# Norm stages of an encoder kernel: one tile at a time with three under way, instead of turns of two tiles

## The chip, the cores and the metric

The kernel runs on one core of one Trainium2 chip. The metric is the device time of one execution in microseconds (us). The core has a matmul engine (TensorE, PE in the rows; PEld is its weight load), a vector engine (VectorE, DVE), a scalar engine (ScalarE, ACT), GpSimd (POOL), and SyncE (SP), which here issues all DMA transfers. Each engine runs its own instructions strictly in order; they meet through semaphores. An instruction that waits holds up all that is queued behind it on its engine.

## The reference, cut to what matters

Two encoder layers run on a prompt of 1024 tokens and a sample of 256 tokens, width 1024, all in float32. Between mixer and MLP the reference norms the sublayer's output, adds it to the residual and norms again:

```python
def rms_norm(x, g, eps=EPS):
    xf = x.astype(jnp.float32)
    y = xf * lax.rsqrt(jnp.mean(xf * xf, -1, keepdims=True) + eps)
    return (y * g.astype(jnp.float32)).astype(x.dtype)
...
        h = rms_norm(x, p['norm_mix_pre'][layer])
...
        x = x + rms_norm(mix, p['norm_mix_post'][layer])
        h = rms_norm(x, p['norm_ffn_pre'][layer])
        f = jnp.square(jax.nn.relu(h @ p['w_ff1'][layer])) @ p['w_ff2'][layer]
        x = x + rms_norm(f, p['norm_ffn_post'][layer])
```

## The kernel before, in words

The 1280 tokens are ten tiles of 128 tokens (partitions) by 1024 features. The kernel is a list of stages, each a block that all engines enter and leave together. Five of the stages are calls of `residual_norm` (L117 to L285), named by tags: norm0 (in front of the input projections; it only norms `x`), norm1, norm2 and norm3 (norm of the sublayer's output, residual add, norm, in one stage), and norm4 (the last residual add; it only does the first half and writes the outputs). In the trace their tiles are called `norm_...` whatever the tag. The other stages, which hold the large matmuls, are not touched.

The tensor `X` (`top_acc`) holds all ten tiles in SBUF. For one tile the full stage does this, in this order:

- ACT squares the sublayer's output with a row sum (L193) and takes the root (L197); DVE takes the reciprocal (L250) and multiplies the tile by it and by the post weight `gpost` (L252); POOL adds the old residual `x_old` (L232), which SP has loaded; SP stores the new residual.
- ACT squares and takes the root again (L207, L211); DVE takes the reciprocal (L258) and scales the rows into `h` (L260); PE turns the eight 128x128 blocks of `h` into PSUM (L282, `norm_ps`); DVE multiplies by the pre weight `gpre`, one value per partition now that the tile is turned, into `h_out` (L267); ACT rounds `h_out` to the high part of the matmul operand (L218); POOL subtracts to make the low part (L239).

The matmuls of the next stage take high and low part, three products for one float32 product.

The order is set by code: `in_turns` runs a hardware loop over turns of two tiles, and in each turn every engine does `begin` (the second norm's root and rows) of turn i, `mixer` (first norm) of turn i+1 and `finish` (turning, high, low) of turn i, each for both tiles of the turn. The small vectors of sums, roots and reciprocals have two columns and are used again each turn. `x_old` is one buffer of two tiles: SP issues its next load when both of its tiles have been added (L153), and the store behind it (L154). norm0 has no mixer and norm4 has only the mixer. The DVE's first arithmetic waits for both weight loads (`n_gains`).

## Time and profile before

| | |
|---|---|
| median of 3 runs | 4993.93 us (4993.36 to 5001.96) |
| the profiled execution | 4994.65 us, its span 4992.9 us |
| PE busy in the span | 4310.9 us (86%) |
| DVE, ACT, POOL busy | 2223.3, 1361.1, 1131.2 us |
| norm0 | starts with the program, next stage's first DMA issue at 74.66 us |
| norm1, norm2, norm3 | from 2138.8, 3109.6, 3954.4 us to 2219.1, 3190.5, 4035.0 us |
| norm4 | from 4925.0 us to the end |

The five stages take about 384 us of the span together, and PE is busy for 76 of these. In the timeline rows a start and a length in us come first, then engine, source line, operation, output and inputs; "x2" is two instructions merged in one row, whose length spans both; what stands in brackets is how long the engine had been idle and what ended that. In the rows by stretch there stand, behind the length, busy time and count of PE, PEld, DVE, ACT and POOL, then the granted PE clock as a share of full speed, the DMA engines' busy share and GB/s. Since stages are separated by a meeting of all engines, a stage's length counts in full.

### The profile page before, as it was taken

Reading aid. Unit: us, or ns where it says so; the run is one execution under the profiler, and the core shown is the slowest. Engines: PE = TensorE matmul, PEld = TensorE weight load, DVE = VectorE, ACT = ScalarE, POOL = GpSimd, SP = SyncE. Lnnn points to the kernel's source line nnn. Section 1 sums busy time; section 2 is a strip of 40 time slices with the busy share of each in tenths; the row PEclk is TensorE's granted clock in tenths of the full one; section 3 lists DMA queues with packets and bytes.
Section 4 is the critical chain, followed back from the end, with each engine's and each line's share of the span. In section 5 each row is a group of like instructions: output and inputs, shape, how many; then the busy total and the mean of one; then the engine's idle time right before and its main releaser. Section 6 shows DMA issues by size and latency. Waiting matters only on the chain. (4 is left out here: it accounts for less than half of the span.)

```text
span 4992.9 us, 65205 instructions
## 1 busy us (share of the span) xinstructions
PE 4310.9 (86%) x24458; PEld 3684.1 (74%) x24458; DVE 2223.3 (45%) x3245; ACT 1361.1 (27%) x2203; POOL 1131.2 (23%) x588
## 2 busy tenths in 40 slices
PE   4989786989999997849999998479999769999994
PEld 3867665888888886738888887357777658888883
DVE  3633044655665555733433443434444233433443
ACT  3211054343333333232111111323333221111111
POOL 2111033343333333351111111400000141111112
PEclk7999767999999998969999999689999879999997
DMA  2222276111111111131111110300000121111102
GB/s 74 73 80 73 64 249 229 52 42 42 59 42 55 42 45 59 45 122 34 42 34 42 35 41 21 98 20 5 5 5 34 47 93 34 42 34 42 40 27 88
DMA packets 211119, 288.09 MB, mean 58 GB/s; under 512 B 36688, under 2 KB 153680, under 8 KB 211040
## 3 DMA queue, kind: packets, MB, share of 16 engines
q1 hardware_dynamic: 211040, 287.05, 17.6%
q8 instruction: 48, 0.79, 0.1%
q14 instruction: 31, 0.25, 0.0%
HBM read 208.37 MB, written 77.99 MB: 57 GB/s over the span
## 5 line engine op out<-in xcount | busy, mean ns | idle before, releaser
L617 DVE TENSOR_TENSOR top_acc<-top_acc,ffn_bank 128x512 f32<-128x512 f32 x640 | 439.9, 687 | 400.0 <-PE ffn_bank L109 400.0
L107 PE MATMUL ffn_bank<-hT_ffn_high,ffn_w_high 128*128 128x512 f32 (+1 forms) x1536 | 545.4, 355 | 32.4 <-DVE ffn_w_low L594 32.4
L108 PE MATMUL ffn_bank<-hT_ffn_low,ffn_w_high 128*128 128x512 f32 (+1 forms) x1536 | 544.9, 355 | 0.0
L109 PE MATMUL ffn_bank<-hT_ffn_high,ffn_w_low 128*128 128x512 f32 (+1 forms) x1536 | 544.8, 355 | 0.0
L108 PE MATMUL ffn_bank<-ffn_w_low,ffn_f_high 128*128 128x512 f32 x1280 | 498.5, 389 | 0.0
L107 PE MATMUL ffn_bank<-ffn_w_high,ffn_f_high 128*128 128x512 f32 x1280 | 498.5, 389 | 0.0
L109 PE MATMUL ffn_bank<-ffn_w_high,ffn_f_low 128*128 128x512 f32 x1280 | 498.1, 389 | 0.0
L609 DVE TENSOR_TENSOR ffn_square<-ffn_relu 128x512 f32<-128x512 f32 (+1 forms) x192 | 146.5, 763 | 662.5 <-ACT ffn_relu L562 662.5
L107 PEld LDWEIGHTS ffn_bank<-hT_ffn_high,ffn_w_high 128*128 128x128 f32 x1536 | 291.4, 190 | 74.6 <-issue 33.2
L232 POOL TENSOR_TENSOR top_acc<-top_acc,norm_x_old 128x1024 f32 (+1 forms) x40 | 111.4, 2804 | 996.6 <-DVE top_acc L252 949.0
L108 PEld LDWEIGHTS ffn_bank<-hT_ffn_low,ffn_w_high 128*128 128x128 f32 x1536 | 291.5, 190 | 41.5
L109 PEld LDWEIGHTS ffn_bank<-hT_ffn_high,ffn_w_low 128*128 128x128 f32 x1536 | 291.3, 190 | 40.3
L586 POOL TENSOR_TENSOR ffn_w_low<-ffn_w_raw,ffn_w_high 128x2048 fp32r<-128x2048 f32 x30 | 138.5, 4615 | 711.3 <-ACT ffn_w_high L568 711.3
L579 POOL TENSOR_TENSOR ffn_w_low<-ffn_w_raw,ffn_w_high 128x2048 fp32r<-128x2048 f32 x32 | 147.1, 4596 | 666.7 <-ACT ffn_w_high L557 666.7
L562 ACT ACTIVATE ffn_relu<-ffn_bank 128x512 f32<-128x512 f32 (+1 forms) x192 | 101.1, 527 | 650.5 <-PE ffn_bank L109 650.5
L109 PEld LDWEIGHTS ffn_bank<-ffn_w_high,ffn_f_low 128*128 128x128 f32 x1280 | 240.3, 188 | 50.0
L107 PEld LDWEIGHTS ffn_bank<-ffn_w_high,ffn_f_high 128*128 128x128 f32 x1280 | 240.4, 188 | 49.1
L108 PEld LDWEIGHTS ffn_bank<-ffn_w_low,ffn_f_high 128*128 128x128 f32 x1280 | 240.4, 188 | 48.8
L282 PE MATMUL norm_ps<-top_ident,norm_h 128*128 128x128 f32 x320 | 75.9, 424 | 221.9 <-DVE norm_h L260 221.9
L557 ACT ACTIVATE ffn_w_high<-ffn_w_raw 128x2048 fp32r<-128x2048 f32 x32 | 61.3, 1917 | 746.8 <-DVE top_acc L617 745.5
L282 PEld LDWEIGHTS norm_ps<-top_ident,norm_h 128*128 128x128 f32 x320 | 63.8, 224 | 233.6 <-DVE norm_h L260 233.6
L1715 POOL TENSOR_TENSOR scan_NM<-scan_NT,scan_both_levels 128x512 f32<-128x512 f32 x120 | 165.0, 1378 | 212.2 <-PE scan_ps L1330 212.2
(388 smaller groups left out, 9402.6 us busy)
## 6 DMA issues: line engine op xcount, KB each, us to landing
ffn_w_raw<-in_w_ff SPq DMA_DIRECT2D x64, 1024.0 KB, 5.1
s_x<-top_acc SPq DMA_DIRECT2D x15, 1024.0 KB, 8.2
norm_x_old<-s_x SPq DMA_DIRECT2D x15, 1024.0 KB, 6.2
s_tm_both<-prepare_tb SPq DMA_DIRECT2D x20, 512.0 KB, 6.8
s_fm_dir<-prepare_fd SPq DMA_DIRECT2D x20, 512.0 KB, 6.4
scan_tb<-s_tm_both SPq DMA_DIRECT2D x20, 512.0 KB, 3.6
scan_fb<-s_fm_both SPq DMA_DIRECT2D x20, 512.0 KB, 4.3
scan_fd<-s_fm_dir SPq DMA_DIRECT2D x20, 512.0 KB, 4.9
```

Source lines behind the costliest of these rows:

```text
L107: pe.matmul(out, stationary[0], moving[0], start=start, stop=False)
L108: pe.matmul(out, stationary[0], moving[1], start=False, stop=False)
L109: return pe.matmul(out, stationary[1], moving[0], start=False, stop=stop)
L232: pool.tensor_tensor(x, x, x_old[:, j:j + 1, :], ALU.add).then_inc(x_updated, 1)
L282: last = pe.transpose(ps[j][:, k, :], h[j][:, k * P:(k + 1) * P], ident[:, :])
L557: act.activation(w2_sb[0][:, :, :], w2_raw[:, :, :], ACT.Copy).then_inc(w2_high, 1)
L562: act.activation(relu[u % 2][:, 0:n], bank[u % 4][:, 0:n], ACT.Relu).then_inc(relu_done, 1)
L579: pool.tensor_tensor(w2_sb[1][:, :, :], w2_raw[:, :, :], w2_sb[0][:, :, :].bitcast(F32), ALU.subtract).then_inc(w2_low, 1)
L586: pool.tensor_tensor(w1_sb[1][:, :, :], w1_raw[:, :, :], w1_sb[0][:, :, :].bitcast(F32), ALU.subtract).then_inc(w1_low, 1)
L609: dve.tensor_tensor(square[u % 2][:, 0:n], relu[u % 2][:, 0:n], relu[u % 2][:, 0:n], ALU.mult).then_inc(squared, 1)
L617: dve.tensor_tensor(a, a, bank[4 + u % 4][:, :], ALU.add).then_inc(added, 1)
L1715: pool.tensor_tensor(NM[u % 2][:, :, :], NTc[q][:, :, :], bcm(both_levels[:, m, :], GR), ALU.mult).then_inc(s["masked"], 1)
```

## The change: what it does

The loops over turns are gone: each stage is written out for ten tiles. In step t every engine does the first norm of tile t+2, the second norm's root and rows of tile t+1, and the high and low part of tile t. Sums, roots and reciprocals have a column per tile. `x_old` is three buffers of one tile, each with a load semaphore of its own; all three loads are issued ahead, and each added tile frees one. The pre weight is loaded broadcast over the partitions (512 KB instead of 4 KB) and applied to the unturned rows, together with the reciprocal, in one scalar_tensor_tensor; the multiply behind the turning and `h_out` are gone. ACT makes the high part straight from PSUM, and DVE, not POOL, makes the low part from PSUM and the high part. POOL has only the residual add left.

```diff
-    mixed = g_post is not None
-    x_old = E.sb("x_old", [P, 2, D])
-    gpost = E.sb("gpost", [P, D])
-    gpre = E.sb("gpre", [P, KB])
+
+    mixed, pre = g_post is not None, g_pre is not None
+    AHEAD = 3
+    x_old = [E.sb(f"x_old{j}", [P, D]) for j in range(AHEAD)]
+    gpost, gpre = E.sb("gpost", [P, D]), E.sb("gpre", [P, D])
...
+            def load(t):
+                dst = x_old[t % AHEAD][:, :] if mixed else X[:, t, :]
+                sp.dma_start(dst, of(x_src, t)).then_inc(loaded[t % AHEAD], 16)
             if mixed:
                 sp.dma_start(gpost[:, :], g_post.partition_broadcast(P)).then_inc(gains, 16)
...
+                for t in range(AHEAD):
+                    load(t)
+            if pre:
+                if not mixed:
+                    load(0)
+                sp.dma_start(gpre[:, :], g_pre.partition_broadcast(P)).then_inc(gains, 16)
             if mixed:
...
+                for t in range(TILES):
+                    sp.wait_ge(x_updated, t + 1)
+                    if t + AHEAD < TILES:
+                        load(t + AHEAD)
+                    sp.dma_start(of(x_dst, t), X[:, t, :]).then_inc(stored, 16)
+                sp.wait_ge(stored, 16 * TILES)
             else:
...
+                for t in range(1, TILES):
+                    if t >= AHEAD:
+                        sp.wait_ge(loaded[t % AHEAD], 16 * (t // AHEAD))
+                    load(t)
...
+            def mix_root_of(t):
+                act.activation(squares[0][:, :], X[:, t, :], ACT.Square, accum_out=col(sq1, t)).then_inc(mix_squares, 1)
+                act.wait_ge(mix_squares, t + 1)
+                act.activation(col(rt1, t), col(sq1, t), ACT.Sqrt, bias=eps[:, :], scale=1.0 / D).then_inc(mix_root, 1)
+
+            def x_root_of(t):
+                if mixed:
+                    act.wait_ge(x_updated, t + 1)
+                else:
+                    act.wait_ge(loaded[t % AHEAD], 16 * (t // AHEAD) + 16)
+                act.activation(squares[1][:, :], X[:, t, :], ACT.Square, accum_out=col(sq2, t)).then_inc(x_squares, 1)
+                act.wait_ge(x_squares, t + 1)
+                act.activation(col(rt2, t), col(sq2, t), ACT.Sqrt, bias=eps[:, :], scale=1.0 / D).then_inc(x_root, 1)
+
+            def high(t):
+                act.wait_ge(turned, t + 1)
+                act.activation(hT[0][part(t)], ps[t % 2][:, :, :], ACT.Copy).then_inc(high_done, 1)
 
-            in_turns(act, begin, mixer, finish)
+            for t in range(-2, TILES):
+                if mixed and t + 2 < TILES:
+                    mix_root_of(t + 2)
+                if pre and 0 <= t + 1 < TILES:
+                    x_root_of(t + 1)
+                if pre and t >= 0:
+                    high(t)
...
+            if mixed:
+                for t in range(TILES):
+                    pool.wait_ge(loaded[t % AHEAD], 16 * (t // AHEAD) + 16)
+                    pool.wait_ge(mix_scaled, t + 1)
+                    pool.tensor_tensor(X[:, t, :], X[:, t, :], x_old[t % AHEAD][:, :], ALU.add).then_inc(x_updated, 1)
...
+            def mixer(t):
+                dve.wait_ge(mix_root, t + 1)
+                dve.reciprocal(col(rc1, t), col(rt1, t)).then_inc(mix_inverse, 1)
+                dve.wait_ge(mix_inverse, t + 1)
+                dve.scalar_tensor_tensor(X[:, t, :], X[:, t, :], col(rc1, t), gpost[:, :], ALU.mult, ALU.mult).then_inc(mix_scaled, 1)
+
+            def rows(t):
+                dve.wait_ge(x_root, t + 1)
+                dve.reciprocal(col(rc2, t), col(rt2, t)).then_inc(x_inverse, 1)
+                dve.wait_ge(x_inverse, t + 1)
+                if t >= 2:
+                    dve.wait_ge(turned, t - 1)
+                dve.scalar_tensor_tensor(h[t % 2][:, :], X[:, t, :], col(rc2, t), gpre[:, :], ALU.mult, ALU.mult).then_inc(h_ready, 1)
+
+            def low(t):
+                dve.wait_ge(high_done, t + 1)
+                dve.tensor_tensor(hT[1][part(t)], ps[t % 2][:, :, :], hT[0][part(t)].bitcast(F32), ALU.subtract).then_inc(low_done, 1)
...
+            dve.wait_ge(gains, 16 * (mixed + pre))
+            for t in range(-2, TILES):
+                if mixed and t + 2 < TILES:
+                    mixer(t + 2)
+                if pre and 0 <= t + 1 < TILES:
+                    rows(t + 1)
+                if pre and t >= 0:
+                    low(t)
...
+            if pre:
+                for t in range(TILES):
+                    pe.wait_ge(h_ready, t + 1)
+                    if t >= 2:
+                        pe.wait_ge(low_done, t - 1)
                     for k in range(KB):
-                        last = pe.transpose(ps[j][:, k, :], h[j][:, k * P:(k + 1) * P], ident[:, :])
+                        last = pe.transpose(ps[t % 2][:, k, :], h[t % 2][:, k * P:(k + 1) * P], ident[:, :])
                     last.then_inc(turned, 1)
```

The functions `in_turns`, `begin` and `finish` go. The two places of the order that matter most, each before and after:

DVE in norm2, from its first arithmetic on, before: `rc1` and `rc2` are the reciprocals of the first and the second norm, `h0` and `h1` the scaled rows of a turn's two tiles; L179 is the start of the loop.

```order
L250 RECIPROCAL norm2_rc1<-norm2_rt1 128x1
L252 SCALAR_TENSOR_TENSOR top_acc<-top_acc,norm2_rc1,norm2_gpost 128x1024
L250 RECIPROCAL norm2_rc1<-norm2_rt1 128x1
L252 SCALAR_TENSOR_TENSOR top_acc<-top_acc,norm2_rc1,norm2_gpost 128x1024
L179 UNCONDITIONAL_BRANCH
L179 ISA
L258 RECIPROCAL norm2_rc2<-norm2_rt2 128x1
L260 ISA
L260 TENSOR_SCALAR norm2_h0<-top_acc,norm2_rc2 128x1024
L257 REGISTER_ALU
L258 RECIPROCAL norm2_rc2<-norm2_rt2 128x1
```

DVE in norm2 after, from the same place on: tiles 0 and 1 mixed, rows of 0; then step 0 (mixer of 2, rows of 1, low of 0) and step 1's mixer.

```order
L217 RECIPROCAL norm2_rc1<-norm2_rt1 128x1
L219 SCALAR_TENSOR_TENSOR top_acc<-top_acc,norm2_rc1,norm2_gpost 128x1024
L217 RECIPROCAL norm2_rc1<-norm2_rt1 128x1
L219 SCALAR_TENSOR_TENSOR top_acc<-top_acc,norm2_rc1,norm2_gpost 128x1024
L223 RECIPROCAL norm2_rc2<-norm2_rt2 128x1
L227 SCALAR_TENSOR_TENSOR norm2_h0<-top_acc,norm2_rc2,norm2_gpre 128x1024
L217 RECIPROCAL norm2_rc1<-norm2_rt1 128x1
L219 SCALAR_TENSOR_TENSOR top_acc<-top_acc,norm2_rc1,norm2_gpost 128x1024
L223 RECIPROCAL norm2_rc2<-norm2_rt2 128x1
L227 SCALAR_TENSOR_TENSOR norm2_h1<-top_acc,norm2_rc2,norm2_gpre 128x1024
L231 TENSOR_TENSOR hT_attention_low<-norm2_ps0,hT_attention_high 128x8x128
L217 RECIPROCAL norm2_rc1<-norm2_rt1 128x1
```

The two mixers of a turn, which stood side by side, are now parted: each mixer is followed by the rows of the tile ahead of it, and each low part stands between a rows and the next mixer.

ACT in norm0 before, the loop over turns (`sq2`, `rt2` sum and root of the second norm); table loads are rows of their own.

```order
L207 ISA
L207 ACT_TABLE_LOAD
L207 ACTIVATE norm0_squares1,norm0_sq2<-top_acc 128x1024
L209 REGISTER_ALU
L207 ISA
L207 ACTIVATE norm0_squares1,norm0_sq2<-top_acc 128x1024
L209 REGISTER_ALU
L211 ACT_TABLE_LOAD
L211 ACTIVATE norm0_rt2<-norm0_sq2,norm0_eps 128x1 x2
L218 ISA
L218 ACTIVATE hT_first_high<-norm0_h_out0 128x8x128
```

ACT in norm0 after, from the stage's start.

```order
L188 ACT_TABLE_LOAD
L188 ACTIVATE norm0_squares1,norm0_sq2<-top_acc 128x1024
L190 ACT_TABLE_LOAD
L190 ACTIVATE norm0_rt2<-norm0_sq2,norm0_eps 128x1
L188 ACTIVATE norm0_squares1,norm0_sq2<-top_acc 128x1024
L190 ACTIVATE norm0_rt2<-norm0_sq2,norm0_eps 128x1
L194 ACTIVATE hT_first_high<-norm0_ps0 128x8x128
L188 ACTIVATE norm0_squares1,norm0_sq2<-top_acc 128x1024
L190 ACTIVATE norm0_rt2<-norm0_sq2,norm0_eps 128x1
L194 ACTIVATE hT_first_high<-norm0_ps1 128x8x128
```

Both table loads stood inside the loop; now both stand ahead of the first root, and none follows in the stage.

## Rows read from the trace of the kernel before

**Rows 1.** Stretches norm0, norm1, norm2 and norm4: length, busy time and count per engine.
```profile
0.00:74.60 74.60, 18.18 (x80) 16.35 (x80) 21.27 (x31) 34.61 (x48) 23.66 (x14) 0.76 0.22 71
2138.80:2219.10 80.30, 19.42 (x80) 15.82 (x80) 41.66 (x51) 37.48 (x70) 53.28 (x20) 0.51 0.42 137
3109.60:3190.50 80.90, 19.43 (x80) 15.82 (x80) 41.66 (x51) 37.47 (x70) 53.69 (x20) 0.53 0.43 136
...
4924.90:4992.90 68.00, 0.00 (x0) 0.00 (x0) 18.57 (x21) 13.89 (x30) 26.26 (x10) 0.51 0.50 162
```

**Rows 2.** Timeline, norm0: start, length, engine, line, what [idle before].
```profile
27.30 0.16 DVE L258 RECIPROCAL norm_rc<-norm_rt 128x1 f32<-128x1 f32 x1 [6.70 <-ACT norm_rt L211]
...
39.86 0.16 DVE L258 RECIPROCAL norm_rc<-norm_rt 128x1 f32<-128x1 f32 x1 [6.70 <-ACT norm_rt L211]
...
68.46 4.66 POOL L239 TENSOR_TENSOR hT_first_low<-norm_h_out,hT_first_high 128x1024 fp32r<-128x1024 f32 x2 [5.21 <-ACT hT_first_high L218]
...
74.66 4.70 SPq L315 DMA_DIRECT2D conv_tap<-in_gdn_conv  x5
```

**Rows 3.** ACT groups, norm0: count | busy, mean ns | idle before.
```profile
L207 ACT ACTIVATE norm_squares<-top_acc 128x1024 f32 (+1 forms) x10 | 10.6, 1055 | 1.0 <-ACT norm_squares L207 0.8
L207 ACT ACT_TABLE_LOAD x4 | 5.1, 1283 | 9.2 <-DMA top_acc<-in_x_prompt 9.1
L211 ACT ACT_TABLE_LOAD x4 | 5.1, 1283 | 0.1
L211 ACT ACTIVATE norm_rt<-norm_sq,norm_eps 128x1 f32<-128x1 f32 x10 | 2.4, 286 | 0.1
L207 ACT ACTIVATION_READ_ACCUMULATOR norm_squares<-top_acc 128x1 f32 x10 | 1.9, 186 | 0.0
```

**Rows 4.** Timeline, norm2, opening and steady loop.
```profile
3109.60 0.38 SPq L145 DMA_DIRECT2D norm_x_old<-s_x  x1
...
3116.90 0.16 DVE L250 RECIPROCAL norm_rc<-norm_rt 128x1 f32<-128x1 f32 x1 [7.16 <-DMA norm_gpre<-in_norm_mix_pre]
3117.10 1.28 DVE L252 SCALAR_TENSOR_TENSOR top_acc<-top_acc,norm_rc,norm_gpost 128x1024 f32<-128x1024 f32 x1
...
3118.49 1.28 DVE L252 SCALAR_TENSOR_TENSOR top_acc<-top_acc,norm_rc,norm_gpost 128x1024 f32<-128x1024 f32 x1
3118.55 5.72 POOL L232 TENSOR_TENSOR top_acc<-top_acc,norm_x_old 128x1024 f32<-128x1024 f32 x2 [58.99 <-DVE top_acc L252]
...
3138.37 0.16 DVE L258 RECIPROCAL norm_rc<-norm_rt 128x1 f32<-128x1 f32 x1 [4.07 <-ACT norm_rt L211]
...
3139.51 1.97 PE L282 MATMUL norm_ps<-top_ident,norm_h 128*128 128x128 f32 x8 [8.73 <-DVE norm_h L260]
...
3144.02 5.75 POOL L232 TENSOR_TENSOR top_acc<-top_acc,norm_x_old 128x1024 f32 x2 [2.32 <-DVE top_acc L252]
3145.17 2.35 DVE L267 TENSOR_TENSOR norm_h_out<-norm_ps,norm_gpre 128x1024 f32<-128x1024 f32 x2
...
3151.58 0.16 DVE L258 RECIPROCAL norm_rc<-norm_rt 128x1 f32<-128x1 f32 x1 [4.06 <-ACT norm_rt L211]
```

**Rows 5.** Timeline, norm4.
```profile
4933.72 6.74 POOL L232 TENSOR_TENSOR top_acc<-top_acc,norm_x_old 128x1024 f32 x2 [58.24 <-DVE top_acc L252]
...
4938.46 3.08 DVE L252 SCALAR_TENSOR_TENSOR top_acc<-top_acc,norm_rc,norm_gpost 128x1024 f32 x1
...
4959.73 4.63 POOL L232 TENSOR_TENSOR top_acc<-top_acc,norm_x_old 128x1024 f32 x2 [6.98 <-DMA norm_x_old<-s_x]
...
4987.26 0.39 SPq L159 DMA_DIRECT2D out<-top_acc  x1
```

**Rows 6.** DMA rate, norm4 and the end of ffn1, in 40 slices.
```profile
GB/s 0 145 420 347 5 0 0 0 0 0 59 356 285 420 95 0 0 74 318 240 416 169 0 0 123 344 287 420 40 0 78 207 266 392 273 0 0 332 275 0
```

**Rows 7.** DMA issues, whole run: count, KB each, us to landing.
```profile
conv_w_raw<-in_w_in_even SPq DMA_DIRECT2D x12, 512.0 KB, 4.5
```

**Rows 8.** Timeline, just before norm1.
```profile
2124.83 1.03 ACT L2062 ACTIVATE top_acc<-gate_ps 128x1024 f32<-128x1024 f32 x1 [10.20 <-PE gate_ps L109]
```

More of the change, by code:

```diff
@@ L187, in _ @@
         @block.scalar
         def _(act):
-            def mixer(i):
-                for j in range(2):
-                    act.wait_ge(mix_scaled, 2 * i + j + 1)
-                    act.sem_inc(tick, 1)
-                    act.activation(squares[0][:, :].unsqueeze(1), X[:, bass.ds(2 * i + j, 1), :], ACT.Square,
-                                   accum_out=sq1[:, j:j + 1]).then_inc(mix_squares, 1)
-                    act.wait_ge(mix_squares, 2 * i + j + 1)
-                for j in range(2):
-                    act.activation(rt1[:, j:j + 1], sq1[:, j:j + 1], ACT.Sqrt, bias=eps[:, :],
-                                   scale=1.0 / D).then_inc(mix_root, 1)
@@ L224, in _ @@
+            act.wait_ge(eps_set, 1)
+            for t in range(-2, TILES):
[5 more added lines that the diff above has]
+                    high(t)
         @block.gpsimd
         def _(pool):
-            def mixer(i):
-                pool.wait_ge(loaded, 16 * i + 16)
-                for j in range(2):
-                    x = X[:, bass.ds(2 * i + j, 1), :]
-                    pool.wait_ge(mix_scaled, 2 * i + j + 1 + 2)
-                    pool.sem_inc(tick, 1)
-                    pool.tensor_tensor(x, x, x_old[:, j:j + 1, :], ALU.add).then_inc(x_updated, 1)
@@ L234, in finish @@
-            def finish(i):
-                for j in range(2):
-                    part = (slice(None), slice(None), bass.ds((2 * i + j) * P, P))
-                    pool.wait_ge(high_done, 2 * i + j + 1)
-                    pool.sem_inc(tick, 1)
-                    pool.tensor_tensor(hT[1][part], h_out[j][:, :, :], hT[0][part].bitcast(F32),
-                                       ALU.subtract).then_inc(low_done, 1)
-            in_turns(pool, lambda i: None, mixer, finish)
+            if mixed:
[3 more added lines that the diff above has]
+                    pool.tensor_tensor(X[:, t, :], X[:, t, :], x_old[t % AHEAD][:, :], ALU.add).then_inc(x_updated, 1)
@@ L244, in _ @@
         @block.vector
         def _(dve):
-            def mixer(i):
-                for j in range(2):
-                    x = X[:, bass.ds(2 * i + j, 1), :]
-                    dve.wait_ge(mix_root, 2 * i + j + 1)
-                    dve.reciprocal(rc1[:, j:j + 1], rt1[:, j:j + 1]).then_inc(mix_chain, 1)
-                    dve.wait_ge(mix_chain, 2 * i + j + 1)
-                    dve.scalar_tensor_tensor(x, x, rc1[:, j:j + 1], gpost[:, :].unsqueeze(1), ALU.mult,
-                                             ALU.mult).then_inc(mix_scaled, 1)
@@ L255, in begin @@
-            def begin(i):
-                for j in range(2):
-                    dve.wait_ge(x_root, 2 * i + j + 1)
-                    dve.reciprocal(rc2[:, j:j + 1], rt2[:, j:j + 1]).then_inc(x_chain, 1)
-                    dve.wait_ge(x_chain, 2 * i + j + 1)
-                    dve.tensor_scalar(h[j][:, :].unsqueeze(1), X[:, bass.ds(2 * i + j, 1), :], rc2[:, j:j + 1],
-                                      None, ALU.mult).then_inc(h_ready, 1)
-            def finish(i):
-                for j in range(2):
-                    dve.wait_ge(turned, 2 * i + j + 1)
-                    dve.wait_ge(low_done, 2 * i + j + 1)
-                    dve.tensor_tensor(h_out[j][:, :, :], ps[j][:, :, :], bc(gpre[:, :], P), ALU.mult).then_inc(scaled, 1)
-                dve.wait_ge(scaled, 2 * i + 2)
```

85 lines of the change are left out of this document (13 added, 72 removed).

## The prediction

> **What bounds the kernel now.** I read the page first: PE is busy 86% of the span, so its idle seventh is what can be won. The view by stretches [rows 1] says where a good part of it lies: norm0, norm1, norm2 and norm4 take 74.6, 80.3, 80.9 and 68.0 us with at most 19.4 us of PE work each (norm3 is another of norm1's kind and within its range). All engines meet at a stage's end, so a microsecond off a stage is one off the program. No engine fills such a stage either: POOL, the fullest, has 53.7 of 80.9 us in norm2. Next the timelines, for what the stages wait on.
>
> In norm0 the same reciprocal comes at 27.30 and 39.86 [rows 2]: 12.6 us for a turn of two tiles. It is one chain through four engines, with DVE idle 6.7 us in front of that reciprocal and two table loads of 1.28 us in each of the four loop turns [rows 3]. In norm2 the turn is 3138.37 to 3151.58, 13.2 us [rows 4]. There POOL is the chain: two adds in 5.75 and later two subtractions, and everybody waits for it in turn. In norm4 POOL ends its two adds in 4.63 us, then stands idle 6.98 us for the reload of its single buffer [rows 5].
>
> One behaviour of the chip decides the rest. A DVE operation with two SBUF tensors of 1024 columns takes 1.28 us [rows 4], but 3.08 us when it starts at 4938.46; POOL's two adds ran from 4933.72 to 4940.46, and the DVE operation ended 1.08 us after them [rows 5]. So it stood still until POOL had finished. POOL pays likewise: two adds cost 4.63 us alone (2.3 each), 6.74 beside DVE. DVE's multiply that reads PSUM takes 2.35 us for two in the midst of POOL's adds [rows 4], so it isn't stopped. The Trainium skill says the same (SBUF — State Buffer, "Who interferes with whom"): a DVE instruction with two SBUF inputs and a GpSimd one that reads SBUF exclude each other for the whole instruction. By that rule, the trace agrees.
>
> **The change part by part.** Durations: mixer and rows 1.28 each, reciprocal with its waits 0.3 before the first and 0.1 between two large ones (3117.10 to 3118.49 is 1.39), transposes of a tile 2.0 [rows 4], square 1.06, read 0.19, root 0.29, so about 1.5 per root with its wait [rows 3], high from PSUM 1.05 [rows 8], low 1.2 (the nearest row is the multiply from PSUM with one SBUF tensor, 2.35 for two [rows 4]; bounds 1.1 and 1.3), add 2.3 alone, a semaphore between engines 0.1 to 0.2.
>
> *norm0.* Gone: six of eight table loads, POOL's subtractions, the multiply behind the turning. Added: rows grow from a multiply by a scalar to 1.28, beside ACT's work. POOL is empty, so nothing stops DVE. What is late next is the chain from high of tile t to high of t+2, since ACT does the root of t+2 right behind high of t: 1.5 root + 0.3 + 1.28 rows + 2.1 turning + 1.1 high = 6.3 for two tiles, 3.15 a tile. DVE needs 2.8 a tile, ACT 2.7, so neither is the bound; the 512 KB loads need about 1.3 at 420 GB/s [rows 6]. Start: before, ACT waits until 9.1 for the first 1 MB [rows 3]; half of it at 420 GB/s is 1.3 less, 7.8 (elsewhere 512 KB land 4.5 after their issue [rows 7], which fits). Two table loads, root and rows give 13.5, the first low ends at 18.1 (turning, the next root in between, high, low). The tenth ends at 18.1 + 9 x 3.15 = 46.5. Before, the last subtraction ends at 73.1 [rows 2]. Gain 26.6 (bounds 22, if half a microsecond more is lost per tile, and 30, if DVE's 2.8 is the pace).
>
> *norm1 to norm3, head.* The pre weight is now 512 KB and is issued behind three residual loads; DVE's first reciprocal waits for it. Before, with 1.5 MB in flight, it comes 7.3 us after the first issue [rows 4]. One MB more at 420 GB/s [rows 6] is 2.5: 9.8. Bounds 7.3 (the queue absorbs it) and 12.3 (half that rate). Then mixers 10.0 to 12.7; add of tile 0 to 15.0 and of 1 to 17.3; rows of 0, held up by the second add, to 18.4; mixer of 2 and rows of 1 to 21.3; add of 2 to 23.6.
>
> *Middle.* Count from the end of add t+1. DVE's mixer of t+2 was waiting for POOL and ends at 1.1. ACT's root of t+1 had to wait for that add, so rows of t+1 can't start before 2.1; POOL, which sees the mixer's semaphore at 1.3, comes first and holds its add to 3.6. Rows end at 4.7, low of t at 5.9. Mixer of t+3 runs 6.2 to 7.5; now the root for rows of t+2 is ready, and rows start 0.1 behind the mixer, before POOL, as 3118.49 stands before 3118.55 [rows 4]. They end at 8.9, low runs beside POOL, POOL's add ends at 11.2, and all begins again. So two tiles cost 11.2 instead of 13.2. Three such pairs bring add of tile 8 to 23.6 + 33.6 = 57.2. *Tail:* add of 9, rows of 8, low of 7, rows of 9, low of 8, transposes, high and low of 9: 12.1, so 69.3. Before, the stretches less the 1.5 from last arithmetic to next issue [rows 2] are 79.4 and 78.8 [rows 1]. Gain 10.1 and 9.5; three times 9.8 is 29.5.
>
> Register instructions of the loops cost nothing visible; POOL's subtractions go from POOL, where they lay on the chain, to DVE, where they lie beside its add. The residual stores (512 KB) end long before the tail does.
>
> *norm4.* Loads are ahead by three tiles, so the 6.98 us waits go; late next is the alternation of DVE and POOL at their shared access: 1.08 + 2.34 = 3.4 a tile. Head as before but with gpost issued first: mixers of 0 and 1 end at 9.4, add of 0 at 11.7, add of 8 at 11.7 + 8 x 3.42 = 39.1, add of 9 at 41.4. From the last store's issue to the end there are 5.6 us for 1 MB [rows 5]; half of it at 420 GB/s is 1.3 less, 4.3. End at 45.9 against 68.0 [rows 1]: gain 22.1. A load and a store per tile are 1 MB, 2.5 us at 420 GB/s and 3.7 at the 285 of middling slices [rows 6], so the loads hide; at 240, also seen there, 4.4 a tile, the gain would be 13.5.
>
> **Sum.** 26.6 + 29.5 + 22.1 = 78.2. From the profiled execution, 4994.65 (1.75 more than its span), that is 4916.4; the median stands 0.7 below it, so 4916.
>
> **The rivals.**
> *POOL first.* POOL always gets in between mixer and rows. The margin that I count on is 0.06 us, and rows has one more wait (for `turned`) than the reciprocal pair it is read from. Then each tile costs mixer 1.28 + 0.2 + add 2.34 + rows 1.08 + low 1.2 + 0.3 = 6.4, add of 2 ends at 22.4, the stage at 22.4 + 45 + 8.4 = 75.6. Three stages then win 10.6 instead of 29.5: 4935. The same page says that who starts first holds the ports to the end; so that order, which no row here fixes for rows against add, decides.
> *DVE first each time.* The pace falls to its floor 1.28 + 0.1 + 1.28 + 2.34 = 5.0 a tile, seven tiles win 4 us a stage, less what the tail takes back: 4906. Against it stands that the root of t+1 must follow the add.
> *The circle closes on each tile: slower.* Low of t holds DVE until ACT's high of t, which is queued behind the root of t+1, which waits for POOL's add, which waits for DVE. If that ring has to be gone round once a tile, it costs add 2.34 + root 1.75 + high 1.1 + low 1.2 + mixer 1.6 + rows 1.6 = 9.6, the stage 23.6 + 67.3 + 12.1 = 103, 24 more than before. Three stages lose 72 against 49 won in the others: 5018. It decides from 8.5 us a tile on. Against it: the code starts each add two tiles ahead, so the ring carries two tiles.
> *The DMA waits stay.* If weights come at 12.3 and norm4 goes by its transfers, 7.5 and 8.6 are lost: 4932.
>
> **How the numbers follow.** Alternating order as above 0.58; POOL first 0.2; DVE first 0.1; DMA waits 0.1; the slower ring 0.02. From 4906 I go down to 4895 for a pace in norm0 and heads at their lower bounds; 4938 takes in POOL first with a little more. A change under 0.2%, 10 us, can hardly be told from none here. All but the ring lie far beyond it, so faster has 0.96, no change 0.015, slower 0.025.
>
> **What would show it.** In norm0 rows repeat every 3.1 to 3.3 us and only two table loads stand at its head. In norm1 to norm3 the first reciprocal comes at about 9.8, the adds come in pairs, one of 2.3 and one of 3.6 to 3.8, and rows alternate between 1.28 and about 2.6; all adds at 2.4 and all rows at 2.6 or more would be POOL first. In norm4 no add waits for a load, and DVE's operations are 2 to 3.4 long. Wrong would be: a norm stage still near 79, or an untouched stage whose matmuls have other lengths than before.

## The result: faster, but just outside the range

The changed kernel took 4939.91 us (median of 4 runs, 4936.71 to 4948.69) against 4994.16 for the kernel before (4993.36 to 5001.96): a ratio of 0.9891, 95% interval 0.9874 to 0.9908. The forecast was 4916, with a range up to 4938, so the median lies 2 us outside it. The profiled execution took 4936.96 us, with a span of 4935.2.

The view by stretches shows where the time went. Columns are those of [rows 1]: length, then busy time and count of PE, weight loads, DVE, ACT and POOL, the granted clock, DMA share and GB/s. Of the changed kernel: norm0, the scan (the recurrences, which the change doesn't touch), norm1, norm2, norm3, norm4.

```profile
0.00:44.66 44.66, 18.55 (x80) 15.12 (x80) 26.00 (x31) 26.12 (x42) 0.20 (x4) 0.73 0.34 131
797.90:1958.40 1160.50, 1032.83 (x8080) 960.99 (x8080) 640.62 (x1030) 414.38 (x661) 422.13 (x319) 0.94 0.15 47
2124.06:2198.00 73.94, 19.69 (x80) 15.69 (x80) 60.11 (x51) 37.99 (x70) 23.45 (x10) 0.50 0.48 156
3088.20:3162.43 74.23, 19.68 (x80) 15.69 (x80) 60.12 (x51) 38.00 (x70) 23.47 (x10) 0.50 0.49 156
3926.40:4000.76 74.36, 19.67 (x80) 15.69 (x80) 60.12 (x51) 39.28 (x71) 23.47 (x10) 0.54 0.49 155
4890.44:4935.20 44.76, 0.00 (x0) 0.00 (x0) 33.28 (x21) 13.45 (x30) 23.41 (x10) 0.51 0.77 246
```

The scan of the kernel before, in the same view:

```profile
831.00:1973.00 1142.00, 1021.40 (x8080) 951.05 (x8080) 653.69 (x1030) 414.27 (x661) 425.75 (x319) 0.95 0.14 47
```

| stage | before | after | difference | forecast |
|---|---|---|---|---|
| norm0 | 74.6 | 44.7 | -29.9 | -26.6 |
| norm1, norm2, norm3 | 80.3, 80.9, 80.7 | 73.9, 74.2, 74.4 | -19.4 | -29.5 |
| norm4 | 68.0 | 44.8 | -23.2 | -22.1 |
| scan | 1142.0 | 1160.5 | +18.5 | 0 |
| all else | | | -3.7 | 0 |
| span | 4992.9 | 4935.2 | -57.7 | -78.2 |

Two things are to be explained: the middle norm stages won 10 us less than forecast, and a stage whose code nobody touched lost 18.5 us. The last stages are the smaller matter: "all else" is spread over the other stages, and such drifts come without a change too (the stage that prepares the tokens was 219.8 to 230.6 us long in the thirteen traces of this study, though no kernel touches it). That is why stage lengths, and not only medians, are compared below.

**The middle stages in the trace.** The timeline of norm2 after the change (start, length, engine, line, what) answers to [rows 4]; its head first, then one tile of the steady part and the start of the next:

```profile
3088.24 0.36 SPq L156 DMA_DIRECT2D norm_gpost<-in_norm_ffn_post  x1
...
3090.06 0.61 SPq L162 DMA_DIRECT2D norm_gpre<-in_norm_mix_pre  x1
...
3097.76 0.16 DVE L217 RECIPROCAL norm_rc<-norm_rt 128x1 f32<-128x1 f32 x1 [9.39 <-DMA norm_gpre<-in_norm_mix_pre]
...
3112.59 1.28 DVE L219 SCALAR_TENSOR_TENSOR top_acc<-top_acc,norm_rc,norm_gpost 128x1024 f32<-128x1024 f32 x1
...
3113.99 3.46 DVE L227 SCALAR_TENSOR_TENSOR norm_h<-top_acc,norm_rc,norm_gpre 128x1024 f32<-128x1024 f32 x1
3114.02 2.34 POOL L211 TENSOR_TENSOR top_acc<-top_acc,norm_x_old 128x1024 f32<-128x1024 f32 x1 [3.75 <-DVE top_acc L219]
...
3117.37 1.21 DVE L231 TENSOR_TENSOR hT_attention_low<-norm_ps,hT_attention_high 128x1024 fp32r<-128x1024 f32 x1
3118.51 0.14 DVE L217 RECIPROCAL norm_rc<-norm_rt 128x1 f32<-128x1 f32 x1
...
3120.08 3.46 DVE L227 SCALAR_TENSOR_TENSOR norm_h<-top_acc,norm_rc,norm_gpre 128x1024 f32<-128x1024 f32 x1
```

The head came out as forecast (first reciprocal 9.5 us after the first issue, 9.8 said). The steady part did not. The rows are recorded 0.03 us ahead of the add, the situation in which the forecast, counting on a margin of 0.06, gave them the shared access, and yet they last 3.46 us and the add 2.34: POOL had the access and DVE stood still. It is so on every steady tile, 6.09 us from rows to rows (3113.99 to 3120.08) instead of 5.6. All 40 adds of the program are short: in the page's list of groups (count | busy, mean ns | idle before)

```profile
L211 POOL TENSOR_TENSOR top_acc<-top_acc,norm_x_old 128x1024 f32<-128x1024 f32 x40 | 93.8, 2345 | 1041.2 <-DVE top_acc L219 1041.2
```

So the rival "POOL first" came true, at 6.1 us a tile instead of its 6.4. Its stage of 75.6 us ends with the last arithmetic; with the 1.5 us from there to the next issue [rows 2] it is 77.1, against 74 measured.

**The scan in the trace.** PE's waits within the scan (engine, what waited <- releaser: us in total, times, longest) begin after the change with the first row below; before the change the same matmuls, then in line 1274, had the second:

```profile
PE scan_ps L1240 <- issue: 25.0, 18, 2.9
```

```profile
PE scan_ps L1274 <- issue: 2.4, 9, 0.3
```

PE is ready and waits for nothing but its own next instruction. In each of nine turns the wait of 0.3 us is joined by one of 2.1 to 2.9 us: 22.6 us more in all. The page's list of DMA queues (packets, MB, share) shows what it fetches, first before, then after:

```profile
q8 instruction: 48, 0.79, 0.1%
```

```profile
q8 instruction: 122, 2.00, 0.2%
```

74 packets more, of 16 KB each. 71 of them fall in the scan, which has 85 instead of 14: some eight per turn.

### The profile page after: what moved, and what is told of

Its sections match the earlier page's. It is cut to its first block and busy times, and to the rows that moved or that the text cites. A ratio compares the mean times of both kernels' runs of the same rounds, so it can differ in the third digit from the quotient of the medians.

```text
span 4935.2 us, 64292 instructions
## 1 busy us (share of the span) xinstructions
PE 4316.5 (87%) x24458; PEld 3686.9 (75%) x24458; DVE 2285.7 (46%) x3245; ACT 1354.3 (27%) x2197; POOL 1013.3 (21%) x548
## 5 line engine op out<-in xcount | busy, mean ns | idle before, releaser
L107 PEld LDWEIGHTS ffn_bank<-hT_ffn_high,ffn_w_high 128*128 128x128 f32 x1536 | 291.3, 190 | 69.3 <-issue 27.9
L211 POOL TENSOR_TENSOR top_acc<-top_acc,norm_x_old 128x1024 f32<-128x1024 f32 x40 | 93.8, 2345 | 1041.2 <-DVE top_acc L219 1041.2
```

The costliest lines, as they stand in the source:

```text
L107: pe.matmul(out, stationary[0], moving[0], start=start, stop=False)
L211: pool.tensor_tensor(X[:, t, :], X[:, t, :], x_old[t % AHEAD][:, :], ALU.add).then_inc(x_updated, 1)
```

## The experiments

Theories: **A**, the change shifted PE's later code and the scan's loop came to lie badly; **B**, the scan lost time to something else. **C**, which of two instructions gets the shared access is a race of a few hundredths of a microsecond, which the recorded starts don't settle, and only operands in SBUF take part in it; **D**, POOL has it whatever is done, or another ring sets the pace. **E** and **F** are on the head, **G** and **H** on the load buffers. Stage lengths, in us:

| kernel | norm0 | scan | norm1, 2, 3 | norm4 | median, runs |
|---|---|---|---|---|---|
| changed kernel | 44.7 | 1160.5 | 73.9, 74.2, 74.4 | 44.8 | 4939.91, 4 |
| a_pad | 60.5 | 1142.5 | 73.9, 74.1, 74.1 | 44.6 | 4938.22, 4 |
| b_pad (of before) | 76.4 | 1158.9 | 80.4, 81.1, 80.8 | 68.0 | 5013.25, 5 |
| e_peloop | 44.7 | 1141.9 | 74.0, 74.1, 74.3 | 45.0 | 4923.15, 4 |
| c_late | 44.6 | 1163.4 | 68.1, 69.0, 68.4 | 42.2 | 4928.89, 4 |
| j_before_direct (of before) | 74.6 | 1141.8 | 85.0, 85.6, 85.4 | 67.1 | 5007.35, 8 |
| d_low | 71.9 | 1162.3 | 77.8, 77.9, 77.7 | 45.0 | 4983.17, 10 |
| f_low1 | 44.8 | 1165.8 | 66.2, 66.1, 66.2 | 45.1 | 4924.41, 4 |
| g_gains | 44.7 | 1163.8 | 69.1, 68.9, 69.0 | 44.8 | 4933.29, 4 |
| h_ahead1 | 44.6 | 1163.1 | 84.7, 83.7, 82.0 | 73.6 | 5005.00, 10 |
| i_ahead2 | 44.6 | 1160.0 | 72.8, 73.1, 72.7 | 44.9 | 4936.28, 4 |
| best | 44.6 | 1143.1 | 61.1, 61.2, 61.2 | 44.6 | 4883.11, 5 |

(norm0 is counted from the span's start to the next stage's first issue, as in [rows 1].) Beside these, the kernel before ran at medians of 4993.58 to 4996.94.

### Code position: a_pad, b_pad, e_peloop

a_pad, in PE's program of norm0, ahead of the turning:

```diff
+            if pre and not mixed:
+                for _ in range(165):
+                    pe.sem_inc(tick, 1)
```

> The changed kernel with 165 semaphore increments more on TensorE ahead of its work in the first norm stage, and nothing else, so that all of TensorE's later code stands 165 instructions further on. Theory A (the change shifted TensorE's code, and the scan's loop now touches a piece of code that has to be fetched again in each turn): with one more shift of that size the loop lies as before, the stage of the scan falls from 1158 to about 1140 us, the packets of the instruction queue from 122 to about 50, the time from 4937 to about 4920. Theory B (the scan lost its 18 us to something else, such as where the DMA engines' work falls or how the stage begins): the scan stays at 1158 within 1 and the time is the same, within 2 us.

Measured: the scan 1142.5, the queue 50 packets, as A said. But the time hardly moved (4938.22, ratio to before 0.9889, 0.9873 to 0.9906), which A had not said. The padding has a price of its own: norm0 is 15.8 us longer. The first transposes start at 28.24 instead of 12.43, since PE works through the increments only once the stage has begun.

```profile
28.24 3.65 PE L255 MATMUL norm_ps<-top_ident,norm_h 128*128 128x128 f32 x16 [28.24 <-issue]
```

The same in the kernel before, ahead of its transposes:

```diff
+            if not mixed:
+                for _ in range(91):
+                    pe.sem_inc(tick, 1)
```

> The kernel before with 91 semaphore increments more on TensorE ahead of its work in the first norm stage, which moves its later code about as far as the change did. Theory A (position of TensorE's code): the scan goes from 1140 to about 1158 us, the packets of the instruction queue from 48 to about 120, the time from 4994 to about 5012. Theory B (something else in the changed stages): no stage changes by over 1 us and the time is the same.

Measured: slower, ratio 1.0038 (1.0023 to 1.0052), scan 1158.9. With none of the change in it, the kernel before takes on the changed kernel's scan, its packets and its wait. The list of queues, PE's waits in the scan, and the first transposes, which started at 15.66 before:

```profile
q8 instruction: 121, 1.98, 0.2%
```

```profile
PE scan_ps L1321 <- POOL scan_e_pos L1699: 23.2, 10, 2.3
PE scan_ps L1277 <- issue: 22.4, 17, 3.3
```

```profile
17.16 3.67 PE L282 MATMUL norm_ps<-top_ident,norm_h 128*128 128x128 f32 x16 [17.16 <-DVE norm_h L260]
```

e_peloop takes the shift back at no cost, by turning in a loop in norm0 (DVE adds 2 to `low_done` at the start, so that no wait is for less than 1):

```diff
-            if pre:
+            if pre and not mixed:
+                with pe.Fori(0, TILES // 2) as i:
+                    for j in range(2):
+                        pe.wait_ge(h_ready, 2 * i + j + 1)
+                        pe.wait_ge(low_done, 2 * i + j + 1)
+                        for k in range(KB):
+                            last = pe.transpose(ps[j][:, k, :], h[j][:, k * P:(k + 1) * P], ident[:, :])
+                        last.then_inc(turned, 1)
+            elif pre:
                 for t in range(TILES):
```

> The changed kernel with TensorE's turning of the rows in the first norm stage written as a loop of five turns of two tiles, so that its later code stands 128 instructions ahead of where the change puts it, with nothing added that takes time. Theory A (position of TensorE's code): the scan falls from 1160 to about 1142 us and the instruction queue's packets from 122 to about 50, as with 165 increments ahead, and the first norm stage keeps its 42 us, so the time is about 4920. Theory B (the 165 increments helped the scan by their delay, not by their number): the scan stays at 1160 and the time at 4937.

Measured: 4923.15, ratio 0.9852 (0.9835 to 0.9868), norm0 unchanged, scan 1141.9, and the row with the releaser "issue" no longer stands at the head of PE's waits. Queues and first wait:

```profile
q8 instruction: 49, 0.80, 0.1%
```

```profile
PE scan_ps L1294 <- POOL scan_e_pos L1672: 23.1, 10, 2.3
```

A holds and B falls. Counted in the built programs, the start of the scan's loop stands, against the kernel before, 98 PE instructions further on after the change, 91 in b_pad, 263 in a_pad, and 30 earlier in e_peloop. Leaving out whole blocks of 256, the slow ones stand at 91 and 98, the quick ones at -30, 0 and 7.

How long the loop is has to be taken from the trace. Its text has 418 matmuls, but the rows count 8080 matmuls and 8080 weight loads in ten turns (nine of the loop and one written out behind it), 808 of each per turn: a float32 matmul stands there as two, a transpose as one. With 78 other instructions (waits, registers, the branch) a turn has about 1700.

The Trainium skill (Runtime: NRT & Kernel Launch, "Instruction fetch mechanics") says that instructions are fetched in blocks of 256, 16 KB each, and that a taken branch to a target outside a window of two such pages makes the engine fetch the target's page first. The block size agrees with the packets (0.79 MB in 48 is 16 KB each), and the long wait for issue comes once in each turn. The window does not agree: 1700 instructions are 6.6 blocks, and the quick kernels run them again and again without fetching (14 packets in the whole scan before).

A loop of 6.6 blocks can lie in seven or in eight. That the eighth is what tells quick from slow fits the five positions and the eight packets per turn; but where the good positions end wasn't measured, so this is argued and not shown. What is shown is that PE's position alone turns the long waits on and off.

### Who gets the shared access: c_late, j_before_direct

The change also took out a line that looks idle: POOL's `sem_inc(tick)` between its wait and its add. c_late puts it back:

```diff
                     pool.wait_ge(mix_scaled, t + 1)
+                    pool.sem_inc(tick, 1)
                     pool.tensor_tensor(X[:, t, :], X[:, t, :], x_old[t % AHEAD][:, :], ALU.add).then_inc(x_updated, 1)
```

> The changed kernel with one semaphore increment on POOL between its wait for the mixer and its add, so that the add is issued one instruction later. Theory C (which of DVE's row operation and POOL's add has the port is decided by a race of a few instructions' time): now DVE's row operation is first wherever its root is ready, shows about 1.2 instead of 3.46 us there, the add 3.6 instead of 2.34, the period falls from 6.1 to 5.0 to 5.6 us per tile, and each of the three middle norm stages becomes 4 to 10 us shorter (time 4907 to 4925). Theory D (POOL's add always gets ahead of what DVE starts within a tenth of a microsecond of it, and what the trace of the kernel before showed there was another case): rows stay at 3.46 and the time is the same or up to 3 us longer. The scan stays at 1158 in both.

Measured: 4928.89, ratio 0.9869 (0.9852 to 0.9885), the middle stages 68.1, 69.0 and 68.4. The timeline of its norm2 (its lines stand two further on) is the alternation of the forecast, add long, then short:

```profile
3115.77 1.28 DVE L229 SCALAR_TENSOR_TENSOR norm_h<-top_acc,norm_rc,norm_gpre 128x1024 f32<-128x1024 f32 x1
3115.83 3.45 POOL L213 TENSOR_TENSOR top_acc<-top_acc,norm_x_old 128x1024 f32<-128x1024 f32 x1 [3.77 <-DVE top_acc L221]
...
3120.52 2.36 POOL L213 TENSOR_TENSOR top_acc<-top_acc,norm_x_old 128x1024 f32<-128x1024 f32 x1 [1.25 <-DVE top_acc L221]
...
3121.02 2.94 DVE L229 SCALAR_TENSOR_TENSOR norm_h<-top_acc,norm_rc,norm_gpre 128x1024 f32<-128x1024 f32 x1
...
3126.59 1.29 DVE L229 SCALAR_TENSOR_TENSOR norm_h<-top_acc,norm_rc,norm_gpre 128x1024 f32<-128x1024 f32 x1
```

The add now stands 0.06 us behind the rows instead of 0.03, and the order is turned round. Where the rows have to wait for ACT's root they start after the add and lose, as forecast. Two tiles take 10.8 us (3115.77 to 3126.59) for the 11.2 of the forecast. The stages moved as C said, by 5 to 6 us; the median is 4 us above C's 4925, and of this the scan, 3 us longer than the changed kernel's, is the larger part.

The other side, in the kernel before:

```diff
                     pool.wait_ge(mix_scaled, 2 * i + j + 1 + 2)
-                    pool.sem_inc(tick, 1)
                     pool.tensor_tensor(x, x, x_old[:, j:j + 1, :], ALU.add).then_inc(x_updated, 1)
```

> The kernel before without POOL's semaphore increment between the wait for the mixer and the add. Theory C (one instruction between wait and work decides who has the port): in the first turn of a middle norm stage POOL's add is now first, 2.34 us instead of 3.6, and DVE's second mixer lasts about 3.46 us instead of 1.28; the adds of a turn end about where they did, so the stages change by under 2 us each. Theory D (which of the two is first does not hang on that instruction): the second mixer of the first turn keeps its 1.28 us and the first add its 3.6.

Measured: slower, ratio 1.0031 (1.0021 to 1.0041). In [rows 4] the second mixer took 1.28 us and the add stood 0.06 behind it. Here, at the same place:

```profile
3119.16 3.46 DVE L251 SCALAR_TENSOR_TENSOR top_acc<-top_acc,norm_rc,norm_gpost 128x1024 f32<-128x1024 f32 x1
3119.20 2.34 POOL L231 TENSOR_TENSOR top_acc<-top_acc,norm_x_old 128x1024 f32<-128x1024 f32 x1 [59.08 <-DVE top_acc L251]
...
3144.68 2.34 POOL L231 TENSOR_TENSOR top_acc<-top_acc,norm_x_old 128x1024 f32 x1 [2.24 <-DVE top_acc L251]
3144.70 3.40 DVE L251 SCALAR_TENSOR_TENSOR top_acc<-top_acc,norm_rc,norm_gpost 128x1024 f32 x1
3148.02 2.34 DVE L266 TENSOR_TENSOR norm_h_out<-norm_ps,norm_gpre 128x1024 f32<-128x1024 f32 x2
```

C holds on who is first. On the price I was wrong: not under 2 us a stage but 4.7. The mixer that is held up holds up what is queued behind it on DVE, the multiply from PSUM (3148.02, where it stood 1.15 us behind the adds' start in [rows 4] and now stands 3.3 behind it), and with it ACT's copies and POOL's subtractions.

### What lies beside the add: d_low, f_low1

If a race decides, the better way is an order without one: put the low part, which reads PSUM, beside the add. d_low swaps low and rows on DVE, and high and the row's root on ACT:

```diff
                     mix_root_of(t + 2)
-                if pre and 0 <= t + 1 < TILES:
-                    x_root_of(t + 1)
                 if pre and t >= 0:
                     high(t)
+                if pre and 0 <= t + 1 < TILES:
+                    x_root_of(t + 1)
...
                     mixer(t + 2)
-                if pre and 0 <= t + 1 < TILES:
-                    rows(t + 1)
                 if pre and t >= 0:
                     low(t)
+                if pre and 0 <= t + 1 < TILES:
+                    rows(t + 1)
```

> The changed kernel with another order in the norm stages: DVE does the mixer of tile t+2, then the low parts of tile t, then the rows of tile t+1; ScalarE the mixer's root, the high parts, then the row's root. The low part (1.21 us, one operand in PSUM) then stands beside POOL's add and the rows after it. Theory C (the port is taken by POOL's add for its 2.34 us and what DVE reads from SBUF waits for it; the low part from PSUM does not): mixer 1.2, low 1.2 beside the add, rows 1.3 after it, period about 4.9 to 5.2 us per tile instead of 6.1, each middle norm stage 8 to 10 us shorter, time 4908 to 4914. Theory D (the low part is held by the add just as the rows are, since its other operand and its result lie in SBUF): it takes about 3.4 us and the period stays near 6.1, time within 3 us of the changed kernel's. The scan stays at 1158 in both.

Measured: worse than either said, 4983.17, ratio 0.9979 (0.9969 to 0.9988). The timeline of norm2 shows why:

```profile
3161.72 2.35 POOL L211 TENSOR_TENSOR top_acc<-top_acc,norm_x_old 128x1024 f32<-128x1024 f32 x1 [3.61 <-DVE top_acc L219]
3162.25 1.02 ACT L194 ACTIVATE hT_attention_high<-norm_ps 128x1024 fp32r<-128x1024 f32 x1 [2.21 <-PE norm_ps L251]
...
3163.31 1.23 DVE L231 TENSOR_TENSOR hT_attention_low<-norm_ps,hT_attention_high 128x1024 fp32r<-128x1024 f32 x1 [1.73 <-ACT hT_attention_high L194]
...
3164.87 1.28 DVE L227 SCALAR_TENSOR_TENSOR norm_h<-top_acc,norm_rc,norm_gpre 128x1024 f32<-128x1024 f32 x1
...
3166.21 1.97 PE L251 MATMUL norm_ps<-top_ident,norm_h 128*128 128x128 f32 x8 [4.00 <-DVE norm_h L227]
```

The low part overlaps the add from 3163.31 and neither is longer for it (1.23 and 2.35): that half of C is right, and D's is wrong. But rows of t+1 now stand behind low of t, which needs high, turning and rows of t: a ring of 5.97 us gone round once a tile, hardly quicker than the changed kernel's 6.09. It holds to the end, where the last low parts still come 6 us apart (3 in the changed kernel), so the middle stages are 3.3 to 3.9 us longer. Norm0, without any adds, pays most for it (71.9 instead of 44.7). My expectation had looked at DVE's queue and not at what low of t needs. It is a mild form of the forecast's slower rival, the circle that closes on each tile.

f_low1 puts the low part of one tile earlier there, in the middle stages only:

```diff
-            for t in range(-2, TILES):
+            for t in range(-2, TILES + 1):
                 if mixed and t + 2 < TILES:
                     mixer(t + 2)
+                if pre and mixed and t >= 1:
+                    low(t - 1)
                 if pre and 0 <= t + 1 < TILES:
                     rows(t + 1)
-                if pre and t >= 0:
+                if pre and not mixed and 0 <= t < TILES:
                     low(t)
```

> The changed kernel with DVE doing, in the three middle norm stages, the low part of tile t-1 between the mixer of t+2 and the rows of t+1; the low part then needs only what was ready long before. Theory C (only operands in SBUF on both engines collide; the low part from PSUM runs beside POOL's add at 1.21 and 2.34 us, and the rows start when the add ends): period mixer 1.47 + add 2.34 + rows 1.28 with gaps, 5.1 to 5.3 us per tile instead of 6.1, each middle norm stage 7 to 9 us shorter, time 4911 to 4916. Theory D (the ring over ScalarE's squares sets the period, not the port): the period stays above 5.8 and the time within 4 us of the changed kernel's. Scan at 1160 in both.

Measured: 4924.41, ratio 0.9858 (0.9841 to 0.9875), although its scan is still the long one. The middle stages are 7.7 to 8.2 us shorter than the changed kernel's, the period 4.97:

```profile
2160.88 1.28 DVE L219 SCALAR_TENSOR_TENSOR top_acc<-top_acc,norm_rc,norm_gpost 128x1024 f32<-128x1024 f32 x1
2162.09 1.22 DVE L231 TENSOR_TENSOR hT_ffn_low<-norm_ps,hT_ffn_high 128x1024 fp32r<-128x1024 f32 x1
2162.31 2.35 POOL L211 TENSOR_TENSOR top_acc<-top_acc,norm_x_old 128x1024 f32<-128x1024 f32 x1 [2.62 <-DVE top_acc L219]
2163.41 2.34 DVE L227 SCALAR_TENSOR_TENSOR norm_h<-top_acc,norm_rc,norm_gpre 128x1024 f32<-128x1024 f32 x1
2165.85 1.28 DVE L219 SCALAR_TENSOR_TENSOR top_acc<-top_acc,norm_rc,norm_gpost 128x1024 f32<-128x1024 f32 x1
```

The rows still collide with the add, but only with its second half: 2.34 us instead of 3.46. The period is just under C's 5.1 to 5.3, at the 5.0 that the forecast named as the floor, and the stages moved as C said. The median is 8 us above C's 4916, of which the scan (1165.8 for 1160) is 6.

### The head and the buffers: g_gains, h_ahead1, i_ahead2

```diff
-                sp.dma_start(gpre[:, :], g_pre.partition_broadcast(P)).then_inc(gains, 16)
+                sp.dma_start(gpre[:, :], g_pre.partition_broadcast(P)).then_inc(gains_pre, 16)
...
             def rows(t):
+                if t == 0:
+                    dve.wait_ge(gains_pre, 16)
...
-            dve.wait_ge(gains, 16 * (mixed + pre))
+            if mixed:
+                dve.wait_ge(gains, 16)
```

> The changed kernel with a semaphore of its own for the second norm weight: the mixers wait for the first weight alone, the first rows for the second. Theory E (the head of each middle norm stage waits for the second of two broadcasts, and that wait is passed on whole): DVE's first reciprocal at about 4.5 instead of 9.4 us after the stage's first issue, each middle norm stage 4 to 5 us shorter, time 4922 to 4925. Theory F (the second broadcast is late for the first rows too, or the loads behind it are, so only the wait moves): stages shorter by under 1.5 us each, time 4933 or more.

Measured: 4933.29, ratio 0.9873 (0.9857 to 0.989), the middle stages 4.8 to 5.4 us shorter. The first reciprocal comes 4.2 us after the stage's first issue (3090.36):

```profile
3094.53 0.16 DVE L217 RECIPROCAL norm_rc<-norm_rt 128x1 f32<-128x1 f32 x1 [4.04 <-DMA norm_gpost<-in_norm_ffn_post]
```

E holds: 5 us of each head was a wait for a weight that nobody needed yet. The median moved by 6.6 us, less than the 15 of the stages and less than E said: this run's scan was 3.3 us longer than the changed kernel's, and the rest lies in other stages that the edit doesn't touch.

h_ahead1 is `AHEAD = 1 if mixed else 3`, i_ahead2 `AHEAD = 2 if mixed else 3`.

> The changed kernel with one load buffer instead of three in the stages that have a mixer. Theory G (the buffers carry the last norm stage and part of the middle ones): each add waits for a load issued when the add before it ended, so a tile takes 2.34 + 4.2 to 5.0 + 0.2 = 6.8 to 7.5 us; the last norm stage goes from 44.8 to about 76 us, the middle ones from 74 to 80 to 86, time 4985 to 5005. Theory H (one buffer is enough where DVE's ring of 6.1 us per tile sets the period): the middle stages keep 74 and only the last becomes longer, time 4965 to 4970.

Measured: 5005.00, a tenth of a percent slower than before (ratio 1.0012, 1.0003 to 1.0022). The groups of POOL in norm4 (us idle and who ended it):

```profile
L211 POOL TENSOR_TENSOR top_acc<-top_acc,norm_x_old 128x1024 f32<-128x1024 f32 x10 | 25.1, 2511 | 93.4 <-DVE top_acc L219 55.0 <-DMA norm_x_old<-s_x 38.4
```

G holds: norm4 28.8 us longer, the middle stages 7.6 to 10.8.

> The changed kernel with two load buffers instead of three in the stages that have a mixer. A load then has a whole tile more than with one buffer: in the middle stages 6.1 + 6.1 - 2.34 = 9.9 us from its issue to its add against a landing of 4.2 to 6 us, so by theory G (a buffer counts only where the landing is longer than what the ring leaves) they keep their 74 us; in the last stage 3.57 + 3.57 - 2.34 = 4.8 us against a landing of 4.2 to 7, so it is 0 to 8 us longer. Time 4937 to 4945. Theory H (the third buffer pays everywhere): middle stages over 2 us longer each, time above 4945.

Measured: 4936.28, ratio 0.9881 (0.9866 to 0.9897), norm4 44.9 and the middle stages even 1.1 to 1.7 us shorter than with three. The second buffer is worth nearly all; the third brings nothing here. Its load stands ahead of the weight's in the queue, and without it norm2's first reciprocal comes 8.6 us after the first issue instead of 9.5. The stage lengths tell this; the medians alone couldn't.

### All that helped: best

e_peloop, f_low1 and g_gains together.

> The changed kernel with the three edits that helped: TensorE's turning in the first norm stage as a loop, the low part of tile t-1 ahead of the rows of t+1 in the middle norm stages, and a semaphore of its own for the second norm weight. If they touch different waits, their gains add: scan 1142 instead of 1160 (-18), each middle norm stage 74.1 - 7.9 - 5.1 = 61 us (-39), time 4937 - 57 = 4880. If the earlier head only meets the loads (a tile of 4.97 us moves 512 KB in and 512 KB out) or the ring over ScalarE, the stages stay at 63 to 66 and the time at 4886 to 4896.

Measured: 4883.11 (five runs, 4882.35 to 4883.38), ratio 0.9779 (0.9766 to 0.9792): 2.2% faster than before, where the changed kernel is 1.1%. The gains add, 61.2 us per middle stage:

```profile
798.70:1941.80 1143.10, 1023.50 (x8080) 953.19 (x8080) 653.09 (x1030) 414.32 (x661) 425.46 (x319) 0.95 0.14 47
2107.40:2168.50 61.10, 19.49 (x80) 15.66 (x80) 52.20 (x51) 37.33 (x70) 23.51 (x11) 0.53 0.57 189
```

## Why the prediction was wrong

**Norm0: right, a little small.** Per tile 3.15 said; rows start at 22.14, 25.54, 28.10, 31.50, 34.07 and 37.47, so 3.1, and from the first low part to the last it is 2.9. Two table loads are left of eight, as said. The first low ended at 16.7 instead of 18.1, since the first table load no longer waits for 1 MB: it started at 6.7, not the 7.8 reckoned. ACT's groups in norm0, against [rows 3]:

```profile
L188 ACT ACT_TABLE_LOAD x1 | 1.3, 1283 | 6.7 <-DMA top_acc<-in_x_prompt 6.7
L190 ACT ACT_TABLE_LOAD x1 | 1.3, 1283 | 0.0
```

**Heads of the middle stages: right** (9.5 for 9.8).

**The pace of the middle stages: the step that failed in the norm stages** is "rows start 0.1 behind the mixer, before POOL, as 3118.49 stands before 3118.55". The row was read rightly, but it belonged to a kernel in which POOL has one more instruction between its wait and its add, and the diff takes that instruction out. c_late and j_before_direct show that this instruction alone turns the order, in either kernel. With it the stage is 68.1, 69.0 and 68.4 us, a little under the forecast's 70.8 (its 69.3 to the last arithmetic and 1.5 to the next issue); without it the rival "POOL first" describes it. Its chance should have been above that of the forecast. The cost against the sum is 10 us, of which norm0's and norm4's better results give back 4. That this rival's time, 4935, lies near the measured one is chance: its three stages are 9 us too slow together, and it has no scan in it.

**Norm4: right in its waits, partly by luck in its sum.** No add waits for a load. The first add ended 8.1 us after the stage's first issue and not 11.7, since `gpost` let DVE begin at 4.2 and the add went ahead of the second mixer. The pace took most of this back: 3.57 us a tile for 3.42, and the last add, too, had to wait for its mixer. The end came 1.1 us earlier than said.

**The term that wasn't there: the step that cost the range.** The sum took every stage outside the norm stages at nothing, without a reason, though the change writes out loops in PE's code. With the scan's +18.5 the sum of the forecast would have been 4935; it is its largest error, and b_pad and e_peloop show both ways that it comes from where PE's code lies. The forecast named as a sign of error "an untouched stage whose matmuls have other lengths than before"; this stage has both, gaps at the issue (22.6 us more) and 11.4 us more of PE busy time. The second follows the first, by the clock. Stretches of one turn, first after the change, behind the long wait, then before it, at the same work:

```profile
956.00:961.00 5.00, 4.83 (x21) 4.54 (x22) 0.79 (x2) 1.20 (x2) 2.27 (x2) 0.50 0.36 108
```

```profile
984.00:987.00 3.00, 3.00 (x16) 3.00 (x16) 1.20 (x3) 1.47 (x3) 0.00 (x0) 0.50 0.35 131
987.00:990.00 3.00, 2.78 (x23) 2.57 (x22) 2.97 (x3) 1.36 (x3) 2.75 (x2) 0.95 0.00 0
```

In both kernels PE's granted clock falls to its lower level (0.50 in the rows, 1.2 GHz) behind a wait of 1.5 us for DVE. Before the change that stretch lasts 3.2 us, and PE works through it without a gap. After the change the long wait falls into it, and it lasts 10 us in this turn and 7 in another (from 1406 to 1413), and the eight matmuls of line 1249 that start at 959.01 take 2.05 us where they took 1.13. Added up over the scan in stretches of 1 us, the lower level holds for 111 us before and in e_peloop, and for 149 to 150 in b_pad and after the change. The two terms are more than 18.5 together, since other waits of PE become shorter by them. Open are where the good positions end and why the badly placed scan is 1158.9 us long in one kernel and 1165.8 in another.

**Buffers.** The forecast gave the DMA waits' end to "three tiles ahead". Two would do.

## What to carry to other kernels

An edit that writes a loop out lengthens the code ahead of every later loop on that engine. So read the instruction queue's packets and the waits for "issue" first when an untouched loop changes its time; turning one stage by a loop again bought 17 us here. When two engines start within 0.1 us of each other on a shared access, count the instructions between wait and work on both sides, of the kernel that is forecast and not of the one that was traced, and better choose an order in which what lies beside the add reads PSUM. And give each load its own semaphore, waited for by its first user.

## What was not expected of the hardware

- A recorded start doesn't tell who has the shared access. DVE's rows recorded 0.03 us ahead of POOL's add stood still for it (3.46 us for 1.28), those 0.06 ahead did not.
- A PE loop of about 1700 instructions costs 2 us more per turn when it lies badly: 18.5 us over the scan. The fetch is only a part of it; PE's clock is at its lower level for 38 us longer.
- A semaphore increment on PE takes about 0.15 us, an estimate from two runs: the engines enter norm0 at 3.0 us, and the first transposes start at 28.24 behind 165 increments (153 ns each) and at 17.16 behind 91 (155 ns each). Padding is not free where the engine is waited for: most of b_pad's lay under the first load, and still norm0 is 1.7 us longer.
